# Experts of a mixture of experts on one Trainium2 core: up products in one piece, the turnings of the inner rows moved behind them

## The reference

```
# tokens sorted by expert (two experts for each token), padded to blocks of 128 rows
def expert_block(args):                  # for each block of 128 rows and its expert e
    xb, e = args
    hb = jax.nn.silu(xb @ w_gate[e]) * (xb @ w_up[e])     # 1024 -> 512
    return hb @ w_down[e]                                 # 512 -> 1024
```

## Time and profile before

| | |
|---|---|
| median of 3 runs | 3533.0 us (3526.64 to 3535.09) |
| the profiled execution's own time | 3526.15 us |
| its span | 3524.5 us |
| TensorE busy | 3210.5 us, 91% |
| VectorE, ScalarE, GpSimd busy | 54%, 39%, 12% |
| mean granted clock of TensorE | 0.948 |
| first and last Silu of the two expert stages, start | 621.3 us, 2152.9 us |

### The profile page before, as it was taken

How to read it: one execution, slowest core, us unless ns; L and a number is a source line. 1 busy time by engine, 2 the same in 40 slices (tenths; PEclk the granted TensorE clock), 3 DMA queues, 4 the chain that set the end, 5 groups by cost and what they waited for, 6 DMA issues and landing times. The chain is left out here.

```text
span 3524.5 us, 49869 instructions
## 1 busy us (share of the span) xinstructions
PE 3210.5 (91%) x19115; PEld 2566.1 (73%) x19115; DVE 1907.9 (54%) x3593; ACT 1373.3 (39%) x2544; POOL 413.8 (12%) x319
## 2 busy tenths in 40 slices
PE   7999997999979989949799998899789989988999
PEld 6895575888858767737688886689655678975557
DVE  5526747658557625665558455622456452325664
ACT  2006732657561133441357456300354320025551
POOL 0100010334320000020133333000100000000000
PEclk9999998999989989979899999999799999988999
DMA  7518124879766200012579667201000221100012
GB/s 212 182 42 264 41 101 162 315 273 392 296 239 198 64 18 1 1 60 108 197 274 372 249 271 284 98 24 37 17 1 1 102 96 32 49 17 1 1 48 109
DMA packets 192931, 462.46 MB, mean 131 GB/s; under 512 B 44147, under 2 KB 119239, under 8 KB 184137
## 3 DMA queue, kind: packets, MB, share of 16 engines
q1 hardware_dynamic: 174281, 392.39, 31.1%
q0 software_dynamic: 18432, 67.12, 5.0%
HBM read 383.41 MB, written 73.33 MB: 130 GB/s over the span
## 5 line engine op out<-in xcount | busy, mean ns | idle before, releaser
L1789 PE MATMUL psum<-high_in,e_rowsT_high 128*128 128x256 f32 (+1 forms) x1080 | 329.9, 324 | 5.5 <-DVE e_rowsT_low L173 5.5
L1790 PE MATMUL psum<-high_in,e_rowsT_low 128*128 128x256 f32 (+1 forms) x1080 | 326.2, 320 | 0.0
L173 POOL TENSOR_TENSOR low_down<-w_down,high_out 128x1024 fp32r<-128x1024 f32 x64 | 205.9, 3234 | 298.9 <-ACT high_out L1867 298.9
L1789 PEld LDWEIGHTS psum<-high_in,e_rowsT_high 128*128 128x128 f32 x1080 | 206.5, 191 | 22.3 <-issue 6.2
L1790 PEld LDWEIGHTS psum<-high_in,e_rowsT_low 128*128 128x128 f32 x1080 | 206.7, 191 | 16.1
L173 DVE TENSOR_TENSOR low_gate<-w_gate,high_in 128x1024 fp32r<-128x1024 f32 x128 | 148.0, 1218 | 7.7 <-ACT high_in L1867 7.5
L3611 DVE CUSTOM_DVE_ANT_0 mla_probs<-psum,mla_mask 128x512 f32<-128x512 f32 (+2 forms) x192 | 96.9, 554 | 99.5 <-PE psum L3476 99.3
L173 DVE TENSOR_TENSOR low_up<-w_up,high_in 128x1024 fp32r<-128x1024 f32 x128 | 148.0, 1218 | 0.0
L1794 PE MATMUL psum<-low_up,e_rowsT_high 128*128 128x256 f32 x720 | 130.5, 283 | 0.0
L1867 ACT ACTIVATE high_out<-w_down 128x1024 fp32r<-128x1024 f32 x128 | 124.7, 1050 | 8.7 <-DMA w_down<-in_exp_w_down 8.7
L1867 ACT ACTIVATE high_in<-w_gate 128x1024 fp32r<-128x1024 f32 x128 | 124.8, 1058 | 6.2 <-issue 6.2
(11 more groups left out here) (596 smaller groups left out, 7792.1 us busy)
## 6 DMA issues: line engine op xcount, KB each, us to landing
w_gate<-in_exp_w_gate SPq DMA_DIRECT2D x32, 2048.0 KB, 8.3
w_up<-in_exp_w_up SPq DMA_DIRECT2D x32, 2048.0 KB, 13.4
w_down<-in_exp_w_down SPq DMA_DIRECT2D x32, 2048.0 KB, 20.1
ada<-in_ada_w SPq DMA_DIRECT2D x24, 1024.0 KB, 6.6
expert_rows<-e_out POOLq DMA_DIRECT2D x47, 512.0 KB, 6.7
expert_rows<-zero_row SPq DMA_DIRECT2D x33, 512.0 KB, 7.0
token_rows<-x SPq DMA_DIRECT2D x32, 512.0 KB, 2.6
x<-token_rows SPq DMA_DIRECT2D x24, 512.0 KB, 6.9
```

What stands on the lines that cost most here:

```text
L173: return eng.tensor_tensor(low, whole, high, ALU.subtract)
L1789: pe.matmul(dst, rows_high[:, k, :], w_high[:, k, cols], start=(k == 0), stop=False)
L1790: pe.matmul(dst, rows_low[:, k, :], w_high[:, k, cols], start=False, stop=False)
```

## The change

Up is made like gate: one call of `enter`, 24 products of 512 columns into one whole bank (`core.bank[1]`). `enter` loses its column range and its `half_way`. `turn_hidden(i, 0)` moves from the middle of up to behind `turn_rows(i + 1)`, right ahead of `turn_hidden(i, 1)`. `up_ready` counts once for a block, and VectorE waits for it once, ahead of half 0. VectorE's instructions and ScalarE's stay as they are.

```diff
-    u_bank = [core.bank[1][:, 0:HALF], core.bank[7][:, 0:HALF]]
+    u_bank = core.bank[1]
...
-            def enter(dst, e, part, cols, half_way=None):
+            def enter(dst, e, part):
...
-                            pe.matmul(dst, rows_high[:, k, :], w_high[:, k, cols], start=(k == 0), stop=False)
-                            pe.matmul(dst, rows_low[:, k, :], w_high[:, k, cols], start=False, stop=False)
+                            pe.matmul(dst, rows_high[:, k, :], w_high[:, k, :], start=(k == 0), stop=False)
+                            pe.matmul(dst, rows_low[:, k, :], w_high[:, k, :], start=False, stop=False)
...
-                            mm = pe.matmul(dst, rows_high[:, k, :], w_low[:, k, cols], start=False, stop=(k == KT - 1))
-                    if half_way and k0 == KT // 2:
-                        half_way()
+                            mm = pe.matmul(dst, rows_high[:, k, :], w_low[:, k, :], start=False, stop=(k == KT - 1))
...
-                    enter(g_bank, e, GATE, slice(0, D_EXPERT)).then_inc(s["gate_ready"], 1)
-                    enter(u_bank[0], e, UP, slice(0, HALF)).then_inc(s["up_ready"], 1)
-                    enter(u_bank[1], e, UP, slice(HALF, D_EXPERT), lambda: turn_hidden(i, 0)).then_inc(s["up_ready"], 1)
+                    enter(g_bank, e, GATE).then_inc(s["gate_ready"], 1)
+                    enter(u_bank, e, UP).then_inc(s["up_ready"], 1)
                     turn_rows(i + 1)
+                    turn_hidden(i, 0)
                     turn_hidden(i, 1)
...
                     for part in range(2):
                         half = slice(part * HALF, (part + 1) * HALF)
-                        dve.wait_ge(s["up_ready"], 2 * i + 1 + part)
-                        dve.tensor_tensor(hid[:, half], hid[:, half], u_bank[part], ALU.mult).then_inc(s["hidden_ready"], 1)
+                        if part == 0:
+                            dve.wait_ge(s["up_ready"], i + 1)
+                        dve.tensor_tensor(hid[:, half], hid[:, half], u_bank[:, half], ALU.mult).then_inc(s["hidden_ready"], 1)
                         dve.wait_ge(s["hid_high_ready"], 2 * i + 1 + part)
```

## The result

| | before | with the change |
|---|---|---|
| median | 3531.64 us (4 runs, 3526.64 to 3535.09) | 3579.97 us (4 runs, 3579.32 to 3581.96) |
| ratio | | 1.0139, 95% interval 1.0121 to 1.0156 |
| span of the profiled execution | 3524.5 us | 3577.7 us |
| from the first Silu's start to the last's | 1531.6 us | 1581.0 us |
| mean granted clock of TensorE | 0.948 | 0.949 |

The kernel is slower by 48.3 us from median to median, 43 to 55 us by the interval. The forecast was 3584, +51.5 us. The spans of the two profiled executions differ by 53.2 us. Of these, 49.4 lie between the first and the last Silu; the ends of 44 of the 45 blocks lie there. Another 1.9 lie ahead of the first Silu (621.3 against 623.2), where the change can't act, and 1.9 behind the last one; the 45th block's end is among these and accounts for 1.2 of them.

What follows compares the result with a forecast made beforehand. TensorE's instruction stream was taken to bound the expert stages: 1.71 us added less 0.52 saved, 45 times, less 2.1 us, gives +51.5 us, forecast 3584 us. Its own range was 3576 to 3593, widened to 3568 to 3600.

Steps and rivals of the forecast that it cites:

- TensorE's stream decides: Expert stages: TensorE's instruction stream sets the time, so each microsecond added or removed counts once for each of 45 blocks.
- Up in one piece saves 0.32 us a block: Up: 24 products of 512 columns take 5.44 us where 48 of 256 take 5.76.
- The chain, 1.85 us: First pair of turnings to first down product, over ScalarE's copy, VectorE's low part, second multiply, second pair: 1.71 us more.
- low part to second multiply: Step on VectorE between the first half's low part and the second multiply: 0.34 to 0.47 us, taken as 0.35.
- The first pair does not wait: Behind the row turnings: first multiply done 0.62 us after the eight row turnings begin, which cover 0.90.
- The four short waits go: TensorE's four waits for the product of gate and up, at the turning in mid-up, vanish: 1.8 us.
- The clock stays: Expert stages: TensorE's granted clock remains 1.00; the rival that it falls had 6%.
- The price I had put on a fall: If TensorE ran at 1.2 GHz behind the turnings: 1.9 us a block, 86 us in all, 3670 us; 6%.
- The sum: Whole kernel: 1.19 us a block over 45 blocks, 53.6 us, less 2.1, gives +51.5 us.
- The range: Whole kernel: 51 to 57 us on runs from 3526.6 to 3535.1, given as 3576 to 3593.
- no chain, and faster: Rival: second multiply runs without waiting for the first half's low part, only the 0.52 us gain stays, 3508 us; 3%.
- breaking up the products: Mid-up: the product behind the first pair of turnings is followed after 0.20 us instead of 0.12; moving them out saves this.

Runs made afterwards that it cites:

- the move alone: Against the kernel before: up stays in two halves, only the first pair of turnings moves behind the next rows' turning; 3595.56 us, ratio 1.0174.
- second experiment: The changed kernel with only VectorE's order altered, both multiplies ahead of the two low parts; 3547.76 us, ratio 1.0041 to before.
- sixth experiment: Against the kernel before: up in two unbroken halves, first pair of turnings right behind up, VectorE's multiplies ahead of the low parts; 3527.39 us, ratio 0.9992.
- seventh: Against the kernel before: up in two unbroken halves, first pair of turnings right behind up, VectorE's order kept; 3555.2 us, ratio 1.0066.
- the fourth: The changed kernel with VectorE's multiplies first and the first pair of turnings behind six of the eight row turnings; 3541.64 us, ratio 1.002 to before.

## Why the prediction was right

*TensorE's stream decides.* Right: the stages got longer by what the block got longer. 44 x 1.18 less the short waits is 49.8 us, and 49.4 lie between the first and the last Silu. A block takes 19.18 us, where 19.2 was forecast.

*Up in one piece saves 0.32 us a block.* Right: 5.45 us for 24 products, 0.227 each, and 12 to 16 us between the move alone and the whole change against 14.4. The gap of N/2.4 + 2.5 ns in the Trainium skill ("TensorE: Matmul & The Clock Gate", Back-to-back issue gap) is given there for an isolated product; by it 2.7 us were to be had, an estimate. It doesn't describe this kernel's stream of products: the trace has 0.227 us for one of 512 columns and 0.120 for one of 256.

*The chain, 1.85 us.* Right in all: 646.97 to 648.82 is 1.85. Its steps are 0.42, 0.41, 0.34, 0.41, 0.06 and 0.21. The step that the trace of before did not show as a sequence, low part to second multiply, came out at 0.34, the lower end. Two of the experiments take the chain out by VectorE's order alone (3579.97 to 3547.76, and 3555.2 to 3527.39), and the move alone keeps it with the wait unchanged. That is the cause, shown from both sides.

*The first pair does not wait.* Right, though with less room than the sum had, 0.19 us instead of 0.28: its multiply was done 0.69 us after the row turnings began, not 0.62, of 0.88.

*The four short waits go.* Right: none is left besides the 45. For these I had 57 us of wait in all; the row says 56.7.

*The clock stays.* Right: 1.00 in both stages, with 0.88 us of row turnings, a pair, 1.26 us of standstill and another pair in each block. The price I had put on a fall never came up. The rule of the Trainium skill ("TensorE: Matmul & The Clock Gate", PE-mode transpose) that such turnings don't count as busy in the way products do is neither borne out nor refuted by this: the stretch without products, 2.73 us here, was followed by products each time, and the clock did not fall.

*The sum.* 51.5 us against 48.3 by the medians, within the interval. In the trace the terms give 49.4 between the Silus and 1.2 for the 45th block, 50.6 together. The range was added up a little loosely: 3526.6 + 51 and 3535.1 + 57 are 3578 and 3592, not 3576 and 3593, and nothing hangs on it. From before's own profiled time it gave 3577.7, where 3579.32 to 3581.96 were measured. That profiled execution was at the low end of before's runs, so the smaller error of this sum is luck.

*Wrong in a rival:* "no chain, and faster" had the point from which it decides, 0.14 us, at VectorE only. The second experiment met its condition to 0.01 us (from the first pair's start to the second multiply's end, 643.92 to 644.07, 0.15 us, and no wait on `e_hidden`) and was still slower than before, because a second chain was behind the first, through ScalarE: down started 1.93 us after up. It was not needed for the forecast, and it is why the 0.52 us per block could not be had by mending VectorE's order alone.

*A term that held here and failed in the sixth experiment:* of the 0.52 us that up was to shrink by, 0.08 were put down to breaking up the products. With the change up does shrink by 0.51 (5.96 to 5.45), so the sum is right; in the sixth and seventh experiments, where the pair stands unbroken between up and the row turnings, it is followed after 0.22 us and the 0.08 come back.

## What to carry to other kernels

When two dependent hand-overs between engines are moved next to each other, look for what made the time between them free before: here eight products and eight turnings covered a round trip over two other engines, which for all but four blocks no row showed as a wait of TensorE. Count that round trip on every engine that it passes, in that engine's own order, against the work that is left in between; the first chain that you remove may only bare a second one. A saving in the number of instructions (0.32 us a block here) is small against one uncovered round trip (1.64 us here, 1.26 of them shown as a standstill).

## What the runs showed of the hardware

- From the end of ScalarE's copy to the first product that uses it lie 0.26 us (644.72 to 644.98 in the second experiment, 648.19 to 648.45 in the fourth), while from VectorE's multiply to the turning lie 0.05 or 0.06, and from ScalarE's copy to VectorE's low part 0.03 (647.77 to 647.80). I had taken all hand-overs for alike; why the first is longer stays open.
- A pair of turnings is followed by the next instruction after 0.14 us in one place (644.39 to 644.53) and after 0.22 in another (644.24 to 644.46 in the sixth experiment), and from a standstill after 0.20 or 0.21 (859.23 to 859.43; 648.61 to 648.82).
- VectorE starts its next instruction 0.08 us before the end of the last also when that one was set going by a wait: 647.80 + 0.42 = 648.22, next at 648.14.
